# A hybrid block kernel on one core: three engines' loops written out, norm squares summed by TensorE, four mask buffers in the scan

## What is computed

```python
a_cs = jnp.cumsum(a, axis=-1)
decay = jnp.where(causal, jnp.exp(a_cs[..., :, None] - a_cs[..., None, :]), 0.0)
cb = jnp.einsum("bclgn,bcsgn->bcgls", cc, bc)
y_diag = jnp.einsum("bcgrls,bcsgrp->bclgrp", cb[:, :, :, None] * decay, xs)
...                                     # prev: state carried into each chunk
y_off = jnp.einsum("bclgn,bcgrpn,bcgrl->bclgrp", cc, prev, jnp.exp(a_cs))
y = (y_diag + y_off).reshape(b, t, h, p) + xh * d_skip[:, None]
```

## Time and profile before

| what | value |
|---|---|
| median of 3 runs | 2393.23 us |
| the profiled execution, device time | 2390.38 us |
| its span, first to last instruction | 2388.6 us |
| TensorE matmul busy | 2270.2 us (95%) |
| VectorE busy | 1475.6 us (62%) |
| ScalarE busy | 1023.3 us (43%) |
| GpSimd busy | 82.8 us (3%) |
| mean granted TensorE clock | 0.989 |

### The profile page before, as it was taken

The page is one execution under the profiler, slowest core; times in us unless marked ns, Lnnn a source line. Parts: engine busy times, 40 slices in busy tenths (PEclk is TensorE's granted clock), DMA queues, the critical chain, the costliest instruction groups (busy, mean ns, idle before and its releaser), DMA issues.

```text
span 2388.6 us, 35770 instructions
## 1 busy us (share of the span) xinstructions
PE 2270.2 (95%) x13256; PEld 1983.1 (83%) x13256; DVE 1475.6 (62%) x1822; ACT 1023.3 (43%) x1436; POOL 82.8 (3%) x53
## 2 busy tenths in 40 slices
PE   7998999898899999999999999999999999999997
PEld 5786777766787788888899999999998988888886
DVE  6757888889966556554656576325448566732545
ACT  5446666643252555532435453223223454422331
POOL 0000001113100000000200000000000000000000
PEclk9999999999999999999999999999999999999998
DMA  3232223212222122233221122222222112222221
GB/s 148 80 111 78 84 99 101 79 71 73 104 71 97 53 97 103 91 123 140 72 92 54 36 89 89 89 88 88 89 88 96 50 54 71 88 106 88 105 89 53
DMA packets 35656, 207.61 MB, mean 87 GB/s; under 512 B 4930, under 2 KB 6978, under 8 KB 12132
## 3 DMA queue, kind: packets, MB, share of 16 engines
q1 hardware_dynamic: 29280, 194.66, 22.5%
q10 hardware_dynamic: 6276, 11.57, 1.6%
HBM read 204.05 MB, written 2.17 MB: 86 GB/s over the span
## 4 chain that ended last, share of the span: by engine, by line
PE 72%; DVE 13%; DVEq 7%; ACT 3%; issue 3%; ACTq 1%; DMA 0%; POOL 0%; POOLq 0%
PE PS L505 22%; PE PS L507 22%; PE PS L509 22%; DVE vout L1831 3%; DVEq L1824 3%; DVE wlo L1602 2%; PE PS L892 1%; ACT whi L1013 1%; PE PS L918 1%; DVEq L1761 1%; DVE hres L1700 1%; DVE xbc L1757 1%; DVEq L1699 1%; PE PS L908 1%; DVE acc L1656 0%
## 5 line engine op out<-in xcount | busy, mean ns | idle before, releaser
L505 PE MATMUL PS<-ahi,whi 128*128 128x512 f32 (+2 forms) x2376 | 734.2, 344 | 17.5 <-DVE xbc L1757 4.9
L507 PE MATMUL PS<-alo,whi 128*128 128x512 f32 (+2 forms) x2376 | 722.0, 339 | 0.0
L509 PE MATMUL PS<-ahi,wlo 128*128 128x512 f32 (+2 forms) x2376 | 720.8, 338 | 0.0
L1602 DVE TENSOR_TENSOR wlo<-raw,whi 128x2048 fp32r<-128x2048 f32 x174 | 398.3, 2289 | 463.4 <-ACT whi L1013 463.3
L1013 ACT ACTIVATE whi<-raw 128x2048 fp32r<-128x2048 f32 x168 | 321.7, 1915 | 672.2 <-PE PS L509 667.0
L505 PEld LDWEIGHTS PS<-ahi,whi 128*128 128x128 f32 x2376 | 414.8, 189 | 81.8 <-issue 30.8
L509 PEld LDWEIGHTS PS<-ahi,wlo 128*128 128x128 f32 x2376 | 414.2, 189 | 48.8
L507 PEld LDWEIGHTS PS<-alo,whi 128*128 128x128 f32 x2376 | 414.4, 189 | 48.3 <-issue 2.0
L505 PE MATMUL PS<-f2hi,whi 128*128 128x264 f32 (+2 forms) x800 | 214.9, 314 | 0.0
L507 PE MATMUL PS<-f2lo,whi 128*128 128x264 f32 (+2 forms) x800 | 214.9, 314 | 0.0
L509 PE MATMUL PS<-f2hi,wlo 128*128 128x264 f32 (+2 forms) x800 | 214.8, 314 | 0.0
(11 more groups left out here) (276 smaller groups left out, 2879.8 us busy)
## 6 DMA issues: line engine op xcount, KB each, us to landing
raw<-weights SPq DMA_DIRECT2D x181, 1024.0 KB, 4.8
acs_b<-acs_rows ACTq DMA_DIRECT2D x34, 256.0 KB, 3.3
const<-const ACTq DMA_DIRECT2D x2, 1232.0 KB, 5.4
x_in<-x_t SPq DMA_DIRECT2D x4, 512.0 KB, 5.1
out_t<-hres SPq DMA_DIRECT2D x16, 128.0 KB, 1.7
cols<-columns SPq DMA_DIRECT2D x1, 385.0 KB, 6.5
const<-const SPq DMA_DIRECT2D x1, 256.0 KB, 6.8
acs_rows<-dtt ACTq DMA_DIRECT2D x1, 64.0 KB
```

Source lines behind the costliest of these rows:

```text
L505: nc.tensor.matmul(o, wh, h, start=first, stop=False)
L507: nc.tensor.matmul(o, wh, h, start=False, stop=False)
L509: mm = nc.tensor.matmul(out[j], wl, hi[j], start=False, stop=last)
L1602: v.tensor_tensor(wlo[s][:, :], raw[s][:, :], whi[s][:, :].bitcast(F32), ALU.subtract).then_inc(lo_ready, 1)
```

## The change

- The scan's loop over the groups is written out on TensorE, ScalarE and VectorE (GpSimd's stays a loop). VectorE's other loops are written out too: xbc, ssm_out, conv_out, ffn_up, ffn_down, and up and down0 of the second block. TensorE's and ScalarE's other loops stay.
- The masks get four buffers, `m_slot[q % 4]`; head q waits for TensorE's head q-4.
- The part of the carried states is no longer added in the bank of the masks' part. TensorE multiplies `st` by the plain C, for two heads at once (128 wide, chunks 1 to 3), into banks 2 and 3. ScalarE's exp(a_cs) fills just the head's 64 partitions and 384 columns of `c_slot[pair % 2]`. VectorE's product L1893 goes; `y_out` multiplies bank 2 or 3 by `c_slot` and adds it after the skip term.
- In the three layer norms TensorE sums all 8 squares; VectorE's copy and adds into `acc1` go, and one `spin(5)` before the sum replaces those between.

```diff
+        m_slot += [at(f"m_slot{s}", vo0 + (2 * s - 3) * TB, T) for s in (2, 3)]
...
+        def units(stage, body, first=0, end=None):
+
+            for u in range(first, stage.n if end is None else end):
+                body(u // 2, u % 2)
...
-                for k in range(1, KD, 2) if pe_odd else ():
-                    spin(9 if k == 1 else 5)
-                    after(pe, n["act"], k + 1)
-                    nc.tensor.matmul(bank(6), ones, sq1[1][:, :], start=(k == 1), stop=False).then_inc(n["pe"].sem, 1)
-                after(pe, n["dve"], summed(pe_odd))
-                nc.tensor.matmul(bank(6), ones, acc1[:, :], start=not pe_odd, stop=True).then_inc(n["pe"].sem, 1)
+                if pe_odd:
+                    spin(5)
+                    for k in range(KD):
+                        after(pe, n["act"], k + 1)
+                        nc.tensor.matmul(bank(6), ones, sq1[k % 2][:, :], start=(k == 0), stop=(k == KD - 1)
+                                         ).then_inc(n["pe"].sem, 1)
...
-            with pe.Fori(0, GROUPS) as g:
+            for g in range(GROUPS):
...
+                        for c in range(1, CHUNKS):
+                            nc.tensor.matmul(bank(2 + j % 2, P, c * P), st[:, (c - 1) * T + j * P:(c - 1) * T + (j + 1) * P],
+                                             cut(xbc, g * T + (CT0 * T + c * P), P), start=True, stop=True)
...
                         mm = nc.tensor.matmul(o, xdt[:, c * T + q * 64:c * T + q * 64 + 64],
-                                              m_slot[hh][:, c * P:(c + 1) * P], start=True, stop=(c == 0))
-                        if c:
-                            mm = nc.tensor.matmul(o, st[:, (c - 1) * T + q * 64:(c - 1) * T + q * 64 + 64],
-                                                  c_slot[hh][:, c * P:(c + 1) * P], start=False, stop=True)
+                                              m_slot[q % 4][:, c * P:(c + 1) * P], start=True, stop=True)
...
-                    if pe_odd and k % 2 and k > 1:
-                        after(act, n["pe"], 1 + k // 2)
+                    if pe_odd and k > 1:
+                        after(act, n["pe"], k)
...
-                    if q >= 2:
-                        hold(act, y_mm, g * GH + (q - 1), "act")
+                    if q >= 4:
+                        hold(act, y_mm, g * GH + (q - 3), "act")
+                    if q >= 4 and s == 0:
+                        hold(act, y_ok, g * GP + (q // 2 - 1), "act")
...
-                    nc.scalar.activation(c_slot[s][:, :], acs_b[s][:, :], ACT.Exp)
+                    r = slice(64 * s, 64 * s + 64)
+                    nc.scalar.activation(c_slot[q // 2 % 2][r, CHUNK:T], acs_b[s][r, CHUNK:T], ACT.Exp)
...
-                    elif k > 1 and (k % 2 or not pe_odd):
+                    elif k > 1 and not pe_odd:
...
-            with dve.Fori(0, GROUPS) as g:
+            for g in range(0, GROUPS):
...
-                    v.scalar_tensor_tensor(t, t, col("ssm_d", g * GP + j), bank(j % 2), ALU.mult, ALU.add
-                                           ).then_inc(y_ok, 1)
+                    e = c_slot[j % 2][:, CHUNK:T]
+                    v.tensor_tensor(e, bank(2 + j % 2, T - CHUNK, CHUNK), e, ALU.mult)
+                    v.scalar_tensor_tensor(t, t, col("ssm_d", g * GP + j), bank(j % 2), ALU.mult, ALU.add)
+                    drain()
+                    t = cut(xbc, g * (GP * T) + (j * T + CHUNK), T - CHUNK)
+                    v.tensor_tensor(t, t, e, ALU.add).then_inc(y_ok, 1)
...
-                    v.tensor_tensor(c_slot[s][:, :], c_slot[s][:, :], cut(xbc, g * T + CT0 * T, T), ALU.mult)
-                    v.tensor_tensor(m_slot[s][:, :], m_slot[s][:, :], cbm[:, :], ALU.mult).then_inc(mc_ok, 1)
+                    m = m_slot[q % 4]
+                    v.tensor_tensor(m[:, :], m[:, :], cbm[:, :], ALU.mult).then_inc(mc_ok, 1)
...
-            with dve.Fori(0, KD // 2) as i:
+            for i in range(0, KD // 2):
```

More of the change, by code:

```diff
@@ L599, in variance @@
             def variance(n, pe_odd=True):
-                for k in range(1, KD, 2) if pe_odd else ():
-                    spin(9 if k == 1 else 5)
-                    after(pe, n["act"], k + 1)
-                    nc.tensor.matmul(bank(6), ones, sq1[1][:, :], start=(k == 1), stop=False).then_inc(n["pe"].sem, 1)
-                after(pe, n["dve"], summed(pe_odd))
-                nc.tensor.matmul(bank(6), ones, acc1[:, :], start=not pe_odd, stop=True).then_inc(n["pe"].sem, 1)
+                if pe_odd:
[4 more added lines that the diff above has]
+                                         ).then_inc(n["pe"].sem, 1)
+                else:
+                    after(pe, n["dve"], summed(False))
+                    nc.tensor.matmul(bank(6), ones, acc1[:, :], start=True, stop=True).then_inc(n["pe"].sem, 1)
             def normed(n):
@@ L1027, in ln_squares @@
                     after(act, n["dve"], centred(k, pe_odd))
[L1028 to L1029 removed]
+                    if pe_odd and k > 1:
+                        after(act, n["pe"], k)
                     nc.scalar.activation(sq1[k % 2][:, :], src[:, k * T:(k + 1) * T], ACT.Square).then_inc(n["act"].sem, 1)
             def ln_std(n, pe_odd=True):
[L1033 removed]
+                after(act, n["pe"], 1 + KD if pe_odd else 2)
                 nc.scalar.activation(std[:, 0:T], bank(6), ACT.Sqrt, bias=col("eps5", 0), scale=1.0 / D
@@ L1160, in _ @@
             stage = PLAN["z_glu"]
-            with act.Fori(0, GROUPS) as g:
+            for g in range(GROUPS):
                 def z_unit(u):
@@ L1621, in layer_norm @@
                         v.scalar_tensor_tensor(t, bank(4), -1.0 / D, t, ALU.mult, ALU.add).then_inc(n["dve"].sem, 1)
-                    if k == 1:
+                    if k == 1 and not pe_odd:
                         after(dve, n["act"], 1)
                         v.tensor_copy(acc1[:, :], sq1[0][:, :]).then_inc(n["dve"].sem, 1)
-                    elif k > 1 and (k % 2 or not pe_odd):
+                    elif k > 1 and not pe_odd:
                         after(dve, n["act"], k)
@@ L1797, in dt_sums @@
                 o.then_inc(dt_ready, 1)
-            unit_loop(dve, stage, xbc_unit, 0, 2)
+            units(stage, xbc_unit, 0, 2)
             dt_ratio()
@@ L1804, in _ @@
             dt_sums()
-            unit_loop(dve, stage, xbc_unit, 4, DT_AT + 2)
+            units(stage, xbc_unit, 4, DT_AT + 2)
             dve.wait_ge(end_ps, 1)
@@ L1808, in _ @@
                                    ).then_inc(end_in, 1)
-            unit_loop(dve, stage, xbc_unit, DT_AT + 2)
+            units(stage, xbc_unit, DT_AT + 2)
             dve.wait_ge(ends_ok, 1)
@@ L1992, in mix_unit @@
                                     ).then_inc(mixlo_ok, 1)
-            unit_loop(dve, stage_c, mix_unit)
+            units(stage_c, mix_unit)
             stage_w = PLAN["w_o"]
@@ L2048, in _ @@
                 up_unit(0, u)
-            unit_loop(dve, stage_u, up_unit, 2)
+            units(stage_u, up_unit, 2)
             stage_d = PLAN["ffn_down"]
@@ L2065, in down_tile @@
                     low(stage_d.slot(1), 4 * i + (stage_d.u0 + 2 * t + 3))
-            with dve.Fori(0, KD // 2 - 1) as i:
+            for i in range(0, KD // 2 - 1):
                 for t in range(2):
@@ L2297, in _ @@
                         up_body(0, s)
-                    unit_loop(dve, stage, up_body, 2)
+                    units(stage, up_body, 2)
                     if h == 0:
-                        unit_loop(dve, PLAN[f"down0_{l}"], lambda i, s: low_next(PLAN[f"down0_{l}"], i, s))
+                        units(PLAN[f"down0_{l}"], lambda i, s: low_next(PLAN[f"down0_{l}"], i, s))
                 stage = PLAN[f"down1_{l}"]
```

15 lines of the change are left out of this document (7 added, 8 removed).

## The result

The changed kernel takes 2360.12 us, the median of four runs (2358.04 to 2362.99); beside it the kernel before took 2392.93 us (2389.94 to 2393.24). The ratio is 0.987, its 95% interval 0.9858 to 0.9881. The profiled execution took 2358.04 us with a span of 2356.2 us, 32.4 us less than the span before. The granted clock is 0.99 in both.

A forecast was written before the change was run, and what follows sets the result against it. TensorE is the full engine, but gains come where it waits for chains through other engines: scan 16.7, ssm_out 6.0, norms 5.2 and 2.5, xbc 0.7, together 31.1 us off 2393.2, forecast 2362.0; 8-in-10 range 2347 to 2379.

The forecast's parts named there:

- ssm_out: Stage after the scan: 28 tap rows on VectorE each save 0.21 us, 6.0 us in all with loop ends, bounds 3 and 8.
- xbc: Stage before the scan: only the last unit's convolution steps lie on the path; four gaps of 0.12 to 0.2, 0.7 us.
- The tap gap: VectorE's single taps in loops start 0.95 us apart, written out 0.83; 0.12 us off each tap, bounds 0 and 0.20.
- The rival in which the gap stays: Writing out saves nothing per tap; a group gains 2.95 us, ssm_out and xbc 0, norms 7.7: 2373.7 us, chance 0.12.
- The scan's group: Each scan group 4.15 us shorter, 63.2 left, bounds 2.5 to 6; scan 16.7 us in all.
- Head 6's new wait: In the scan, ScalarE's head 6 waits for `y_out(1)`; covered by 3 us before VectorE wants exp 6.
- 1.0 from the four buffers: In the scan, ScalarE's head 2 no longer waits 1.08 us for TensorE, so ScalarE gains 1.0 us.
- TensorE hides the other units: In xbc, gains in all units but the last are covered by TensorE's work and give nothing.
- Norms: Squares and matmuls alternate over two buffers: roots 2.6 us earlier in two layer norms, 2.5 us in the input norm.
- The clock rival: Gaps between squares in the norms halve TensorE's clock: 2381 us with all three norms, 2368 to 2375 with fewer; chance 0.08.
- more than forecast: Head 3 isn't late (7 us) and the clock stays up before the convolution's mean (1.5): 2353 us, chance 0.13.
- Fetching: Rival: written-out code needs 40 to 50 more instruction packets; stalls of 0.85 us each would give 2400 us, chance 0.04.

## Why the prediction came true, step by step

The predicted time was 2362.0 us and the measured one 2360.1. The sum of 31.1 us stands against 32.4 in the traces. That it came out within 1.3 us is in part luck: ssm_out was put 2.8 us too high and the norms 0.7, while xbc was put 2.2 too low, the scan 1.1, and 1.5 us came from stages that the sum leaves out.

- **The tap gap** (0.12 taken, bounds 0 and 0.20). Right: pitch 0.83. The rival in which the gap stays, 2373.7 us, is refuted by these rows, and the two pairs of kernels that differ in the scan's loops alone show that it reaches the time: 2377.8 against 2393.0, and 2360.1 against 2374.4. The form of the code does change the time between the same instructions. The pairs are not the tap gap alone: seven table loads of ScalarE and its shorter issue times go with the loops.
- **The scan's group** (4.15 us, 63.2 left). Measured 4.2 and 4.5, and 63.0; only the first group, at 5.0, gained more. The steps came as forecast too: counted from the second x products (334.87 before, 320.20 after), head 3's product is 2.3 us earlier (359.51, 342.54; forecast 2.2) and head 7's 3.5 (381.16, 362.96; forecast 3.5). ScalarE late for head 3 "for about 1.2 to 1.8 us": 1.45, and 0.31 at head 2. Issue time between heads 0.3 less: 0.40. `y_out` 1.15 more: from its first product (343.15) to the next tap (345.08) it takes 1.93, and 0.84 with the old order written out, so 1.09. Head 6's new wait was to be covered by 3 us: it was 2.33 and covered by 4.2. One thing went on record wrongly: I credited "1.0 from the four buffers". With two buffers the period is the same and head 2 starts without a wait (337.60, timeline of ScalarE in that kernel), so the relief came from TensorE being through with head 0 earlier, not from the added buffers.
- **ssm_out** (6.0 us, measured 3.2, bounds 3 and 8). Mis-sized, in two parts. First, the row of three: I read "2.07 for a row counted by starts" out of 4.22 us for six taps. A row's start to start is 4.22 less the last row's width of 2.08, so 2.14, and the gain on the earlier trace rows 0.14 and not 0.21: 3.9 us for 28 rows. Without GpSimd's sums the stretch gained 4.5. Second, the sums: beside them VectorE runs at GpSimd's pace and the gap was hidden already, which left 3.0. I had noted the doubled taps in the scan and forgotten them in ssm_out. "TensorE's own slack is above 6 us, so it follows" was true but was not what limited the gain.
- **xbc** (0.7 us, measured 2.9). Wrong in "TensorE hides the other units". It does so up to about 132 us, and after that four steps of ScalarE's copies take 43.86 us instead of 45.86 (134.37 to 180.23 before). I had looked at TensorE's busy share and not at which wait ended last in a unit.
- **Norms** (2.6 twice and 2.5). 2.4, 2.3 and 2.4. The cycle of square, matmul and square over two buffers was the right model: ScalarE starts every second square 1.90 us apart (746.27, 748.17, 750.08), forecast 1.85. The clock rival did not come: in windows of the kernel after (columns as in the earlier trace rows) the clock is full in the norm, and even just behind the convolution's mean, where the earlier trace rows had 0.58. (The prediction quotes for a full clock; they print none, but the window from 769 to 782 us of the kernel before has 1.00.)

```profile
620.00:624.00 4.00, 3.36 (x14) 2.15 (x13) 2.37 (x4) 2.55 (x3) 0.00 (x0) 1.00 0.10 39
622.00:626.00 4.00, 3.95 (x16) 2.95 (x17) 2.61 (x2) 2.34 (x3) 0.00 (x0) 1.00 0.02 4
742.00:753.00 11.00, 10.20 (x32) 4.63 (x33) 5.29 (x9) 6.73 (x11) 4.54 (x1) 1.00 0.27 95
```

TensorE's wait before the convolution's mean is 0.64 us now and was 2.61. This part of the case "more than forecast" came, but not its 1.5 us: from this mean to the mean of the norm after w_o it is 120.42 us now and was 120.69.
- **Fetching** (40 to 50 packets more). The queues carry 11 more, and no wait of the kind shows: the idle time before the weight loads of the first pass that has "issue" as its cause is 44.2 us after and 48.8 before. The Trainium skill's statement (Runtime: NRT & Kernel Launch, § Instruction fetch mechanics) that straight code is fetched ahead agrees with that.

## What to carry to other kernels

Read the cost of a hardware loop off one and the same instruction in both forms of code, start to start, and count it for every instruction of the body, not for the most frequent one. Then ask for each stretch whether something else sets the pace there: an engine that shares it with VectorE hides the gap, and work given to GpSimd can cost VectorE more than doing it. After a gain, the new wait that the trace names is the next step: the 1.76 us a group for two exp rows were worth 8.4 us in all with one move of lines.

## What the hardware showed that I had not expected

- Four sums on GpSimd stretch nine taps of VectorE from 6.38 to 10.38 us; the 24 sums cost 21.4 us, 19.0 in the stretch and 2.4 before its first row (509.74 - 454.33 = 55.41 against 507.52 - 454.51 = 53.01), where the same taps on VectorE cost 16.1 (24 x 0.67).
- ScalarE's 7 fewer instructions after (1436 to 1429) are table loads. Four of them stand at L1204 before, one in each group, and the loop form of the changed kernel has 1436 again: the looped body repeats loads each turn that the written-out code does without. The Trainium skill (ScalarE activation tables: per-element evaluation and per-set limits, § Table sets in the compiler and the runtime) says that the loads are placed block by block, which these counts agree with. From the last exp of head 2 to head 3's first row, with the issue of a DMA between, ScalarE stands idle 0.86 us in the loop and 0.46 with fixed addresses.
- VectorE's own time in a group stayed 59.7 to 59.9 us in three written-out kernels with different orders of work, and 64.7 to 65.0 in two looped ones. So the loops cost VectorE 5 us of 65, and little of that depends on the order of work.
